# Matrix products of a mixture of experts in another order: each of the three products for both column halves in turn

## The reference

```
y_lat = jnp.concatenate([..., ...], axis=-1) @ w_out          # 1024 x 1024, latent (and, in layer 0, context) tokens
x_lat = x_lat + mod[2] * y_lat
aff = jax.nn.softmax((h @ w_router).astype(jnp.float32), axis=-1)
g, idx = lax.top_k(jnp.swapaxes(aff, 1, 2), cap)               # 128 latent tokens for each expert
xg = jax.vmap(lambda hb, ib: hb[ib])(h, idx)
hid = jax.nn.silu(jnp.einsum('becd,edf->becf', xg, w_gate)) * jnp.einsum('becd,edf->becf', xg, w_up)
out = jnp.einsum('becf,efd->becd', hid, w_down) * g.astype(h.dtype)[..., None]
```

## Time and profile before

| | |
|---|---|
| Time, median of 3 (lowest to highest) | 2594.79 us (2594.1 to 2595.84) |
| The profiled execution: its time, its span | 2593.67 us, 2591.8 us |
| Mean granted TensorE clock | 0.959 of full speed |
| Busy: PE, PEld, DVE, ACT, POOL | 2362.2, 1811.6, 1783.2, 1415.4, 204.1 us |
| Matrix instructions | 13256 |
| Moved by DMA | 585.56 MB, mean 226 GB/s |

### The profile page before, as it was taken

One profiled execution on the slowest core, in us unless ns is written; L12 is line 12 of the kernel. 1 busy time (PEld: TensorE's weight loads), 2 busy tenths in 40 slices (PEclk: granted clock), 3 DMA queues, 4 the chain that ended last, 5 costly groups with the idle time before them and its releaser, 6 DMA issues.

```text
span 2591.8 us, 34527 instructions
## 1 busy us (share of the span) xinstructions
PE 2362.2 (91%) x13256; PEld 1811.6 (70%) x13256; DVE 1783.2 (69%) x1987; ACT 1415.4 (55%) x1440; POOL 204.1 (8%) x220
## 2 busy tenths in 40 slices
PE   6999998789849999999999968988984999999994
PEld 4887776568736666666666647876864788888883
DVE  5523212454587888888888767566658899999995
ACT  6310112664526566666656654557353777777774
POOL 0000000000010111211111010000000011111110
PEclk9999999899969999999999989999997999999997
DMA  6034546545317877887887861112345999999995
GB/s 246 25 106 133 164 146 126 220 181 203 122 55 279 290 290 280 291 302 291 291 305 280 305 198 29 29 37 77 123 177 193 352 380 398 390 388 387 388 377 182
DMA packets 194342, 585.56 MB, mean 226 GB/s; under 512 B 19657, under 2 KB 64449, under 8 KB 187713
## 3 DMA queue, kind: packets, MB, share of 16 engines
q1 hardware_dynamic: 178688, 529.61, 54.8%
q0 software_dynamic: 12336, 48.24, 7.2%
q10 hardware_dynamic: 3216, 6.29, 0.7%
HBM read 536.88 MB, written 47.21 MB: 225 GB/s over the span
## 4 chain that ended last, share of the span: by engine, by line
PE 84%; DVE 6%; ACT 5%; DMA 3%; issue 2%; SPq 0%; POOL 0%; ACTq 0%; POOLq 0%; DVEq 0%
PE ps L1588 14%; PE ps L1590 13%; PE ps L1589 13%; PE ps L1603 6%; PE ps L571 5%; PE ps L572 4%; PE ps L573 4%; PE ps L796 3%; PE ps L798 3%; PE ps L797 3%; PE ps L508 1%; PE ps L608 1%; PE ps L542 1%; PE ps L610 1%; PE ps L609 1%
## 5 line engine op out<-in xcount | busy, mean ns | idle before, releaser
L1814 DVE TENSOR_TENSOR R_H_r<-R_M,R_W_r 128x2048 fp32r<-128x2048 f32 x336 | 758.9, 2287 | 140.9 <-ACT R_W_r L1716 138.6
L1716 ACT CAST R_W_r<-R_M 128x2048 fp32r<-128x2048 f32 x336 | 640.0, 1916 | 215.6 <-PE ps L1590 214.5
L1590 PE MATMUL ps<-R_W_r,R_C_r 128*128 128x512 f32 x1536 | 605.4, 394 | 0.0
L1588 PE MATMUL ps<-R_W_r,bc_r 128*128 128x512 f32 x1024 | 411.3, 402 | 5.8 <-ACT R_W_r L1716 2.9
L1589 PE MATMUL ps<-R_H_r,bc_r 128*128 128x512 f32 x1024 | 402.9, 393 | 0.0
L1590 PEld LDWEIGHTS ps<-R_W_r,R_C_r 128*128 128x128 f32 x1536 | 288.4, 188 | 65.9
L1588 PEld LDWEIGHTS ps<-R_W_r,bc_r 128*128 128x128 f32 x1024 | 192.2, 188 | 65.4 <-issue 10.9
L571 PE MATMUL ps<-R_H_r,R_W_r 128*128 128x512 f32 (+1 forms) x632 | 232.4, 368 | 4.9 <-ACT R_W L2177 2.0
L572 PE MATMUL ps<-R_C_r,R_W_r 128*128 128x512 f32 (+1 forms) x632 | 229.0, 362 | 0.0
L573 PE MATMUL ps<-R_H_r,R_W_r 128*128 128x512 f32 (+1 forms) x632 | 228.7, 362 | 0.0
L1589 PEld LDWEIGHTS ps<-R_H_r,bc_r 128*128 128x128 f32 x1024 | 192.3, 188 | 42.5
(11 more groups left out here) (322 smaller groups left out, 3769.5 us busy)
## 6 DMA issues: line engine op xcount, KB each, us to landing
R_M<-in_moe_w_gate SPq DMA_DIRECT2D x114, 1024.0 KB, 8.4
R_M<-in_moe_w_down SPq DMA_DIRECT2D x112, 1024.0 KB, 8.1
R_M<-in_moe_w_up SPq DMA_DIRECT2D x110, 1024.0 KB, 7.4
bc<-in_ada_w SPq DMA_DIRECT2D x28, 1024.0 KB, 4.9
R_H<-in_moe_w_up SPq DMA_DIRECT2D x18, 1024.0 KB, 7.2
R_H<-in_moe_w_down SPq DMA_DIRECT2D x16, 1024.0 KB, 8.8
R_H<-in_moe_w_gate SPq DMA_DIRECT2D x14, 1024.0 KB, 7.8
R_W<-in_ev_w_in SPq DMA_DIRECT2D x25, 512.0 KB, 3.9
```

Source lines behind the costliest of these rows:

```text
L1588: pe.matmul(o, hi[:, k, :], wh[:, kk, cs], start=(k == 0), stop=False)
L1590: ins = pe.matmul(o, lo[:, k, 0:P], wh[:, kk, cs], start=False, stop=(k == KC - 1))
L1716: nc.scalar.copy(whi[j], raw[slot + j]).then_inc(unit_high_done, 1)
L1814: nc.vector.tensor_tensor(wlo[j], raw[slot + j], whi[j], ALU.subtract).then_inc(unit_low_done, 1)
```

## The change

In both places the loop over the two column halves moves inside each product. In place of `hi x wh`, `hi x wl`, `lo x wh` for half 0 and then the same three for half 1, TensorE makes `hi x wh` for half 0 and half 1, then `hi x wl` for both, then `lo x wh` for both. Instructions, operands, waits and counts are the same ones; only their order changes.

```diff
@@ pe_wout
-                        for c in range(2):
-                            o, cs = ps[:, 4 + 2 * (i % 2) + c, :], slice(c * BANK, (c + 1) * BANK)
-                            xh, xl = cathi_of[l][i % 2][:, k, :], catlo[l][:, k, i * P:(i + 1) * P]
+                        xh, xl = cathi_of[l][i % 2][:, k, :], catlo[l][:, k, i * P:(i + 1) * P]
+                        out = [(ps[:, 4 + 2 * (i % 2) + c, :], slice(c * BANK, (c + 1) * BANK)) for c in range(2)]
+                        for o, cs in out:
                             pe.matmul(o, xh, wh[:, cs], start=(k == 0), stop=False)
+                        for o, cs in out:
                             pe.matmul(o, xh, wl[:, cs], start=False, stop=False)
+                        for o, cs in out:
                             ins = pe.matmul(o, xl, wh[:, cs], start=False, stop=(k == KC - 1))
@@ pe_moe, unit
+                    half = [slice(c * BANK, (c + 1) * BANK) for c in range(2)]
                     for c in range(2):
-                        o, cs = ps[:, bank + c, :], slice(c * BANK, (c + 1) * BANK)
-                        pe.matmul(o, hi[:, k, :], wh[:, kk, cs], start=(k == 0), stop=False)
-                        pe.matmul(o, hi[:, k, :], wl[:, kk, cs], start=False, stop=False)
-                        ins = pe.matmul(o, lo[:, k, 0:P], wh[:, kk, cs], start=False, stop=(k == KC - 1))
+                        pe.matmul(ps[:, bank + c, :], hi[:, k, :], wh[:, kk, half[c]], start=(k == 0), stop=False)
+                    for c in range(2):
+                        pe.matmul(ps[:, bank + c, :], hi[:, k, :], wl[:, kk, half[c]], start=False, stop=False)
+                    for c in range(2):
+                        ins = pe.matmul(ps[:, bank + c, :], lo[:, k, 0:P], wh[:, kk, half[c]], start=False, stop=(k == KC - 1))
```

## The result

| | before | changed |
|---|---|---|
| Median of 20 runs, us | 2593.81 | 2597.77 |
| Lowest and highest, us | 2590.4, 2598.32 | 2593.32, 2601.76 |
| Ratio of the runs, 95% interval | | 1.0016 [1.001, 1.0021] |
| Span of the profiled execution, us | 2591.8 | 2595.6 |

The change makes the kernel slower by 0.16%, some 4 us. The prediction was 2591.2 us, 3.6 us faster than the 2594.79 us that were known then. The size of the change lies inside 0.2%, but the interval excludes no change, and the sign is the other one.

The account below looks back on a forecast made before the run. A full TensorE was taken to bound the kernel. Terms 0 + 0 - 1.6 - 2 = -3.6 us against the profiled 2593.67 us gave 2590.1, as median of runs 2591.2 us; full range 2579 to 2603.

Parts of the forecast that it names:

- What bounds the kernel: In experts and projections, a full TensorE: time is the number of matmuls times the distance between two starts.
- D: Rival on TensorE's clock: it falls to its lower level for a tenth of touched matmuls; +109 us, 2704 us; chance 0.02.
- Banks at 0: All 5472 touched matmuls: alternating the bank after one matmul in place of three costs 0 ns.
- Projections at 0: Projection tiles, 864 matmuls: 0.7 ns above the floor, 0.6 us in all, taken as 0.
- Gate and up, -2 us: Gate and up, 256 units: of a total excess of 16.6 us, the new order saves 2 us.
- The second reading: Gate and up: excess goes with every load, saving nothing; the first reading, with changes of block, would save 8.3 us.
- Down, -1.6 us: Down matrix, 128 units: half the steps to and from `lo` go, and half the excess with them; -1.6 us.
- rival C: Gate and up: the two new kinds of step cost 0.24 us each; +8.1 us, 2602.9 us; chance 0.17.
- Rival A: Gate, up and down: the excess goes with changes of block everywhere; -9.9 us, 2584.9 us; chance 0.22.
- rival B: All touched matmuls: a repeated stationary block is swapped in for nothing; -24.4 us, 2570.4 us; chance 0.04.

Follow-up runs that it names:

- down_banks: Kernel before, but in the down matrix alone the bank alternates after every matmul, with the old sequence of stationary blocks; 2595.4 us, ratio 1.0007.
- rest_alone: Kernel before, with gate, up and the output projections in the new order and down in the old one; 2593.25 us, ratio 1.0002.
- hi_and_lo_off_128: aligned_old with 40 words of padding behind `bc` and gate's and up's low blocks moved by 32 words, both 128 bytes off; 2592.08 us, ratio 0.9996.
- down_blocks: Kernel before, but down alone takes the new sequence of stationary blocks, with banks 0, 0, 1, 1, 0, 1; 2596.61 us, ratio 1.0017.
- aligned_new: Changed kernel with all low blocks at a step of 128 words and 8 words of padding behind `bc`; 2577.97 us, ratio 0.9946 to the kernel before.
- aligned_old: Kernel before, old order, with all low blocks at a step of 128 words and 8 words of padding behind `bc`; 2578.39 us, ratio 0.9952.
- hid_step_old: Kernel before, old order, with down's low blocks at a step of 128 words in place of 160; 2589.9 us, ratio 0.9992.

## Why the prediction was wrong

**What bounds the kernel**: right. TensorE is full, the time is matmuls times distance, and no wait appeared; the clock stayed at 1.00 (D did not happen).

**Banks at 0**: right, shown by down_banks, rest_alone and the two aligned kernels.

**Projections at 0**: right, 0.2272 us.

**Gate and up, -2 us**: the measured value is 0 (5.58 against 5.57 us for 24); this term was mis-sized. The second reading, that the excess goes with every load of an off-grid block and not with the changes, held whole in gate and up; the lean towards the first had no row behind it.

**Down, -1.6 us**: this is the step that failed. "Half of these steps go, so half of the excess does" took the excess for a fixed price of each change to or from `lo`. In the kernel before it does sit at these steps (233 and 234 ns beside 227), but the price did not stay fixed. The excess of a unit went from 0.025 to 0.06 us over the whole matrix (0.08 in the middle units) instead of to 0.0125, +4.5 us in all. The step from low to low costs 241 ns and the one behind it 240, and the excess spread to even k, in which every block is on the grid. The place of the blocks was rightly seen as the cause: with the low blocks on the grid the excess is gone in both orders. But hi_and_lo_off_128 shows an excess without any change of place between stationary blocks, and down_blocks that the same six matmuls behind the same blocks cost more when the two low ones stand together. A count of changes can't give that. The sequence lo, lo had no row of before, so its price should have been bounded in down as well, as in rival C: at the 0.24 us of the earlier trace rows for the two new kinds of step, 512 steps x (0.24 - 0.2288) = +5.7 us, close to what came. That it is so close is luck: only the step from low to low in odd k takes 0.24, and most of the loss is in the even k. I had put rival C in gate and up alone, where it did not happen.

**Rival A** (excess goes with changes) and **rival B** (repeats come free): both excluded; aligned_new has twice the repeats of aligned_old and takes the same 2.73 us a unit. The Trainium skill ("TensorE: Matmul & The Clock Gate", Part 2, "Step-by-step: what each phase is for") says that a load apart from the matmul lets one load once and multiply repeatedly. The order alone gains nothing of that here, since each matmul keeps its own load, 13256 for 13256.

**Small slips**: the prediction says that every stream has 226.7 ns a matmul; by its own rows gate and up have 232.1. And its chances of C and D add up to 0.19, where it has 0.18 for slower.

## What to carry to other kernels

On a full TensorE read the distance between starts, stream by stream, averaged over many matmuls; two streams of the same shape that differ tell of something worth more than their order. Here it was the place of the stationary block against the moving operand: 8 words of padding and a step of 128 words in place of 160 brought 14 us, where reordering the same matmuls brought nothing or a loss. In a kernel like this one, put the operands on one grid before reordering, then see whether there is anything left to order.

## What the runs showed of the hardware that I had not expected

- At a granted clock of 1.00 a matmul of 512 columns in this format with a load of its own starts 0.2267 us after the one before, when its stationary block and the moving operand start a multiple of 256 bytes apart. A unit of 12 takes 2.72 us then (aligned_old, aligned_new, down in hid_step_old); with `hi` 64 bytes off 2.75, with `hi` 128 bytes off 2.80, with `hi` and `lo` both 128 bytes off 2.79.
- The order of matmuls with off-grid blocks changes the price even of neighbours whose blocks are on the grid (even k of down, 1.36 to 1.40 us; single steps of 224 to 236 ns in place of 227).
- Which bank a matmul writes had no effect at 512 columns, and on the grid neither had whether its stationary block is the same as the last one's. What in the chip makes the place count was not shown.
